# Spreading the later modulation tiles of a transformer block by TensorE's time per weight tile

## The reference

```python
mod = silu(c) @ w_ada + b_ada          # 2048 x 12288, six parts of 2048
sh1, sc1, g1, sh2, sc2, g2 = split(mod)
h = rmsnorm(x) * (1 + sc1) + sh1       # hc: the same for the context
p = h @ w_in                           # K, V, F (Fourier), Q, two gates
q, k = rope(rmsnorm(q)), rope(rmsnorm(k))
o = softmax(q k_all^T / sqrt(128)) v_all      # 16 heads, 4 of K and V
y = (sigmoid(g_a) * (o @ w_attn_o) + sigmoid(g_f) * (fft2(f).real @ w_fourier)) @ w_out
x = x + g1 * y
x = x + g2 * (relu((rmsnorm(x) * (1 + sc2) + sh2) @ w1) ** 2 @ w2)
return rmsnorm(x)
```

## Time and profile before

| | |
|---|---|
| median of 3 runs | 1567.03 us (1566.25 to 1568.39) |
| the profiled execution | 1566.27 us |
| its span | 1564.5 us |
| PE busy | 1514.5 us, 97% |
| DVE busy | 927.6 us, 59% |
| ACT busy | 672.1 us, 43% |
| mean granted TensorE clock | 0.991 |

### The profile page before, as it was taken

The page is one execution under the profiler, slowest core; times in us unless marked ns, Lnnn a source line. Parts: engine busy times, 40 slices in busy tenths (PEclk is TensorE's granted clock), DMA queues, the critical chain, the costliest instruction groups (busy, mean ns, idle before and its releaser), DMA issues.

```text
span 1564.5 us, 19384 instructions
## 1 busy us (share of the span) xinstructions
PE 1514.5 (97%) x7009; PEld 1205.6 (77%) x7009; DVE 927.6 (59%) x1042; ACT 672.1 (43%) x931; POOL 25.5 (2%) x38
## 2 busy tenths in 40 slices
PE   4999999999999999999998999999999999999996
PEld 1446888878788887887876888888888888888885
DVE  1336675777676668788878545444445555455556
ACT  2324333645544454433445344444444444444443
POOL 0000100101000000000000000000000000000001
PEclk8999999999999999999999999999999999999998
DMA  9999587776676679978973666666555655555561
GB/s 338 329 344 332 184 308 232 257 252 202 196 233 222 200 249 320 317 276 310 346 283 110 189 188 190 197 181 184 182 171 189 198 195 192 193 194 190 194 198 78
DMA packets 108538, 357.61 MB, mean 229 GB/s; under 512 B 11072, under 2 KB 12096, under 8 KB 107584
## 3 DMA queue, kind: packets, MB, share of 16 engines
q1 hardware_dynamic: 106288, 351.32, 67.3%
q10 hardware_dynamic: 2192, 5.51, 0.9%
HBM read 354.68 MB, written 2.10 MB: 228 GB/s over the span
## 4 chain that ended last, share of the span: by engine, by line
PE 89%; DMA 5%; DVE 3%; ACT 2%; issue 1%; POOL 1%; ACTq 0%; SPq 0%; DVEq 0%; POOLq 0%
PE bank L1212 27%; PE bank L1214 27%; PE bank L1213 27%; DMA raw<-in_w_ada 3%; PE bank L1348 2%; PE bank L1330 2%; PE bank L1374 1%; PE bank L1450 1%; PE bank L1338 1%; DVE wl L911 1%; ACT wh L587 1%; DMA raw<-in_w_out 1%; PE bank L1244 1%; PE bank L1268 0%; PE bank L1302 0%
## 5 line engine op out<-in xcount | busy, mean ns | idle before, releaser
L911 DVE TENSOR_TENSOR wl<-raw,wh 128x1024 fp32r<-128x1024 f32 x464 | 563.9, 1224 | 498.8 <-ACT wh L587 497.7
L587 ACT ACTIVATE wh<-raw 128x1024 fp32r<-128x1024 f32 x464 | 486.0, 1059 | 459.1 <-PE bank L1214 442.2
L1212 PE MATMUL bank<-wh,hT 128*128 128x512 f32 x512 | 208.8, 408 | 3.8 <-DVE wl L911 2.0
L1212 PE MATMUL bank<-wh,h2T 128*128 128x512 f32 x512 | 202.5, 396 | 2.4 <-DVE h2T L1098 2.4
L1214 PE MATMUL bank<-wh,hT 128*128 128x512 f32 x512 | 201.0, 393 | 0.0
L1213 PE MATMUL bank<-wl,hT 128*128 128x512 f32 x512 | 200.0, 391 | 0.0
L1214 PE MATMUL bank<-wh,h2T 128*128 128x512 f32 x512 | 199.8, 390 | 0.0
L1213 PE MATMUL bank<-wl,h2T 128*128 128x512 f32 x512 | 199.4, 389 | 0.0
L1212 PE MATMUL bank<-wh,hidS 128*128 128x512 f32 x512 | 199.3, 389 | 0.0
L1214 PE MATMUL bank<-wh,hidS 128*128 128x512 f32 x512 | 199.2, 389 | 0.0
L1213 PE MATMUL bank<-wl,hidS 128*128 128x512 f32 x512 | 199.2, 389 | 0.0
(11 more groups left out here) (168 smaller groups left out, 1496.2 us busy)
## 6 DMA issues: line engine op xcount, KB each, us to landing
raw<-in_w SPq DMA_DIRECT2D x256, 512.0 KB, 4.3
raw<-in_w_ada SPq DMA_DIRECT2D x192, 512.0 KB, 5.6
raw<-in_w_in SPq DMA_DIRECT2D x128, 512.0 KB, 4.5
raw<-in_w_attn_o SPq DMA_DIRECT2D x32, 512.0 KB, 5.7
raw<-in_w_out SPq DMA_DIRECT2D x32, 512.0 KB, 6.2
raw<-in_w_fourier SPq DMA_DIRECT2D x16, 512.0 KB, 6.1
xt<-in_x ACTq DMA_DIRECT2D x2, 1024.0 KB, 8.9
ct<-in_ctx ACTq DMA_DIRECT2D x2, 1024.0 KB, 14.2
```

Of the source, the lines that this page charges most:

```text
L587: nc.scalar.activation(slot, raw[:, s % RAW, :], ACT.Copy).then_inc(wh_done, 1)
L911: nc.vector.tensor_tensor(lo, raw[:, s % RAW, :], hi.bitcast(F32), ALU.subtract)\
L1212: nc.tensor.matmul(bank[b][:], a_hi, w_hi, start=first, stop=False)
```

## The change

Only the rule that fills `ADA_AT` and `STREAM` is changed. A unit is now 0.8 in K and V, 0.5 in F, 0.9 in Q, 1 in A and GF1's end, 0.85 in B, 0.9 in O, and 1.3 for the tiles from Q1's tile 8 to GF1's tile 13 (`ATTENTION`). The 128 tiles are divided by the sum of these units over all tiles but the last five, which gives 0.641 modulation tiles per unit and so 0.833 per tile in the attention, where it was 0.62. Modulation tiles by chunk, before and after: K 2 and 1, V 10 and 4, F 10 and 5, Q0 9 and 9, Q1 10 and 12, GA0 10 and 13, GA1 10 and 13, GF0 10 and 14, GF1 10 and 13, A0 10 and 10, B0 5 and 4, A1 10 and 11, B1 5 and 4, O0 10 and 9, O1 7 and 6. The column sums stood behind F's tile 7, Q1's 1, GA0's 10, GF0's 4 (these four give columns, L1268), GF1's 14 and A0's 3, A1's 0 and 5; they now stand behind Q0's 10, GA0's 1, GA1's 5, GF0's 8, GF1's 11 and A0's 0, B0's 3 and A1's 0.

```diff
--- before.py
+++ after.py
@@ -111,12 +111,21 @@
 STREAM = []
 ADA_AT = {}
 ADA_END = {}
+PACE = {"K": 0.8, "V": 0.8, "F": 0.5, "Q": 0.9, "G": 1.0, "A": 1.0, "B": 0.85, "O": 0.9}
+ATTENTION = range(TILES.index(("Q1", 8)), TILES.index(("GF1", 14)))
+
+
+def pace(m):
+    return 0.0 if m < MODS_END + 2 else 1.3 if m in ATTENTION else PACE[TILES[m][0][0]]
+
+
+PER_UNIT = 128.0 / sum(pace(m) for m in range(M1 - 5))
 _units, _n = 0.0, 0
 for _m, (_name, _k) in enumerate(TILES):
     STREAM.append(("M", FETCH[_m], 0))
-    _units += 0.0 if _m < MODS_END + 2 else 2.0 if _name in "KV" else 1.0
+    _units += pace(_m)
     ADA_AT[_m] = []
-    while _n < 128 and _n < _units * 0.62:
+    while _n < 128 and _n < _units * PER_UNIT:
         ADA_AT[_m].append(_n)
         STREAM.append(("A", _n // KT, _n % KT))
         if _n % KT == KT - 1:
```

## The result

The changed kernel takes 1574.9 us (median of 4 runs, 1572.93 to 1576.06); the kernel before, run beside it, 1567.49 (4 runs, 1566.25 to 1568.39). The ratio is 1.0048 [1.0033, 1.0063]: slower by 7.4 us, more than the 0.2% that can be told. (A ratio and its 95% interval are taken over all runs of both kernels, and can differ by up to 0.0008 from the quotient of the two medians. Of the 24 executions of the kernel before that stand beside the first experiments one took 3092.27 us; it is in their median of 1567.32 and in no ratio.) The forecast was 1572.4, in a range of 1565.5 to 1578.5, with a chance of 0.75 for slower.

A forecast was written before the change was run, and what follows sets the result against it. PE, busy 97% of the span, was taken to bound the kernel. -0.6 + 1.7 + 1.4 + 4.6 - 1.7 = +5.4 us on 1566.27 gave 1571.7; with 0.76 for the median, 1572.4 us, range 1565.5 to 1578.5.

The forecast's parts named there:

- The turns: DVE-ScalarE loop in the attention: 5.70 us plus 1.20 per modulation tile, so 6.89 with one, 8.09 with two.
- Units 5 to 31: Attention from GA0 on: two-tile turns exceed PE's pace of 7.67 us, lateness becomes PE waits; +4.6 us.
- The second way of adding: Units 5 to 31 summed by turns: 215.0 us less 2.4 unpaid lateness, PE 212.6 against 207.74; +4.9 us.
- End of Q1: Q1's tile 8 to GA0's tile 0: two more modulation tiles delay Q1's evacuation; +1.4 us.
- Start of Q1: Column sum leaves Q1's tile 1; only DVE's wait for it comes back; -0.6 us.
- GA0's start: The column sum moved to GA0's tile 1 costs its full time, as lateness is small there; +1.7 us.
- the clock: Rival: PE waits drop the clock, 1.7 us each, three make +5.1, 1577.5 us; chance 0.15 with other waits.
- B1 and O0: Ends of B1 and O0: the modulation tile ahead of the evacuation goes, and PE's wait with it; -1.3 and -0.4 us.
- other work covers the lateness: Rival: DVE's spare third in the attention takes the 11 more tiles; -4.8 us, 1562.2 us; chance 0.08.
- Half is hidden: Rival: lateness limits looser, or GA0's rotations start with room; +2 to +3 us, about 1569.5 us; chance 0.17.
- A new wait on the DMA: Rival: transfers hold up the attention, same size as the clock rival; chance 0.15 shared with the slow clock.

The follow-up runs named there:

- the late sum: Changed kernel with the second modulation part's column sum put back behind GA0's tile 10 instead of tile 1; 1574.43 us, ratio to before 1.0047.
- The second table: Kernel with modulation tiles per turn set by hand, two column sums moved and A1, B1, O1 begun without a modulation tile; 1561.48 us, ratio to before 0.997.
- the added loads: Kernel before with 16 unused loads of 512 KB added from GA0's tile 6 to GF1's tile 3; 1566.23 us, ratio 0.9994.
- the added work: Kernel before with eleven DVE reductions of a constant added between units 5 and 31, no transfers; 1573.2 us, ratio 1.0039.
- the first table: Kernel with modulation tiles per turn set by hand in place of the rule, before two sums and three counts were mended; 1568.38 us, ratio to before 1.0014.

## Why the prediction was right

It forecast +5.4 us and slower; the medians differ by 7.4. By its own steps:

*The turns.* Predicted were 8.09 us with two modulation tiles and 6.89 with one. Reductions of GA1 in the changed kernel, with the wait for the high part between them:

```profile
466.70 0.68 DVE L1037 TENSOR_REDUCE mx<-bank 128x1 f32<-128x512 f32 x1
...
470.12 1.23 DVE L920 TENSOR_TENSOR wl<-raw,wh 128x1024 fp32r<-128x1024 f32 x1 [1.94 <-ACT wh L596]
...
474.79 0.68 DVE L1037 TENSOR_REDUCE mx<-bank 128x1 f32<-128x512 f32 x1
...
481.68 0.68 DVE L1037 TENSOR_REDUCE mx<-bank 128x1 f32<-128x512 f32 x1
```

474.79 - 466.70 = 8.09 and 481.68 - 474.79 = 6.89. In the rotations of GA0 the reductions of DVE's timeline start at 363.43, 373.78, 382.93, 393.27 and 403.61: turns of 10.35, 9.15, 10.34 and 10.34 us, where 10.34, 9.15, 10.34 and 10.34 were predicted.

*Units 5 to 31.* PE took 212.2 us where it took 207.74, +4.5; forecast was +4.6. The kernels without a wait in this stretch, which hold two column sums there like both of these, take 205.1; so the changed kernel lost 7.1 us (reckoned 7.6) and the kernel before 2.6 (reckoned 3.2). Both were half a microsecond too high, and that cancels in the difference. The waits lie a little otherwise: 2.9 at the end of GA0 (forecast 2.6), 0.4 over the end of GF0 (8.09 us from scores to scores for 7.67, forecast 1.1), and the other 3.8 in GA0 (forecast 3.9) as small waits, none of which is shown longer than 0.5. The second way of adding had 215.0 us between the reductions and 2.4 of lateness left at the end; measured were 214.2 and 1.9. The Trainium skill's rule in Perfetto Trace Analysis, Identifying the Most-Contended Engine, which takes an engine's occupancy for how near VectorE is to its limit, would have made this term 0. Here DVE was busy 44.72 of 63.40 us in GA1, and the turn still passed PE's pace; the measurement decides against it for this loop.

*End of Q1.* +1.4 forecast, +1.4 measured: the wait for `qraw` went from 0.9 to 2.3.

*Start of Q1.* -0.6 forecast, -0.8 measured.

*GA0's start* is the term that was mis-sized: +1.7 for the moved sum, and +3.4 measured from GA0's first product to the scores of unit 5. The sum is 1.8 of it (9.51 us from the scores of unit 4 to those of unit 5, for 7.67). The other 1.6 are the clock: 0.50 from 348.66 to 352.07, right behind the wait of 2.3 us, about half of 3.41 us lost. This is the rival "the clock" in part: one such time in the chunks, not three. It is read from one execution, and the kernel with the late sum had the same wait without it; so how often it falls there is open.

*B1 and O0.* -1.3 and -0.4 forecast, -0.8 and 0 measured. At the end of B1 the timeline of DVE shows why, against the earlier trace rows:

```profile
738.30 1.28 DVE L940 SCALAR_TENSOR_TENSOR acc<-raw,cc,acc 128x1024 f32<-128x1024 f32 x1
739.72 1.23 DVE L920 TENSOR_TENSOR wl<-raw,wh 128x1024 fp32r<-128x1024 f32 x1
740.86 2.48 DVE L1068 SCALAR_TENSOR_TENSOR gateF<-gateF,bank 128x512 f32<-128x512 f32 x4
```

The modulation tile has only moved one weight tile forward, and still presses a little on the evacuation: the wait is 0.4, not 0. (The second table has no tile behind either of these two weight tiles, and no such wait.) At O0 the wait of 0.4 for `scr` stayed without a modulation tile ahead of it, so the tile had not been its cause: DVE's additions begin 1.8 us ahead of O1's first product in both kernels (780.34 and 782.09 before, 785.49 and 787.26 now), and now it is PE's last product that releases them.

*What the sum had not got.* -0.5 in A0, B0 and A1, where the column sums that give rows stand at other tiles; no run shows which of that saves it. And +1.5 behind O1, with one more stretch at clock 0.50 (843.60 to 847.00) at the step to the MLP. Such a stretch came at that step in seven of the eight other profiles of edited kernels too, at changing places, and not in that of the kernel before; no edit goes with it. All together: -0.8 + 1.4 + 3.4 + 4.5 - 0.8 - 0.5 = 7.2, the difference of V to the end of O1.

The rival "other work covers the lateness" fell with the turns of 8.09 us. "Half is hidden" fell with the +4.5. A new wait on the DMA was not there, and with sixteen loads more it still wasn't.

## What to carry to other kernels

Where two engines hand work to each other once per step, read the length of a turn from start to start of the same instruction, and set it against the pace of the engine that bounds: an idle third in the busy shares is no room if it lies inside the turn. What is added must then be counted per turn, not per microsecond of the stage, and a repair can be to shorten the turn, by putting what doesn't depend on it (here the next tile's rounding) ahead of the wait; here that was one edit of a few lines, and it kept every modulation tile in its place. Whoever moves work by a formula should look at where the things that hang on its counts (here the column sums) come to stand.

## What the runs showed of the hardware

Between Q1 and GF1 the clock fell to 0.50 in six of the ten kernels, once in each, mostly for 3.4 us and near the end of a wait of PE: behind 0.8 us before and with the added loads, 2.3 in the changed kernel, 2.0 with the added work (clock 0.51 from 398.5 to 401.9) and, for 6.8 us, behind the 2.1 of the late sum. With the first table it fell at 400.25, in the last half microsecond of the wait of 2.5. The falls behind a wait began 0.2 to 2.5 us after its end. It did not fall behind the wait of 2.9 at the end of GA0 (the window of GA1 shows 1.00), nor behind the same 2.3 for `qraw` when the sum stood late. At the step to the MLP, where every kernel waits 2.6 us for `xs` and then 1.6 to 2.4 for `h2T`, eight of the ten profiles show one fall, of 3.4 or 6.8 us, and those of the kernel before and of the late sum show none. So the length of the wait right ahead does not decide it alone, and what else does stays open. In the four kernels whose GA0 has no such wait, GA0 took 65.3 us at a clock of 1.00. The Trainium skill, TensorE: Matmul & The Clock Gate, HAM oscillation, describes a kernel throttled again and again by its waits; the traces agree that waits stand at the falls, but they show single falls, not a repeated one.

The denser stream cost nothing that could be seen: with the loads added the DMA share was 0.79 in GA1, GA0 and GA1 were as long as before to 0.1 us, and the ratio was 0.9994.
